# Forget gates and step sizes as extra columns of the first value products

## What is computed

```python
def fox_mixer(h, w_in, b_forget, w_out):          # the "odd" mixer, 16 heads
    q, k, v, fz = _split(h @ w_in, ODD_SPLITS)    # 1024, 1024, 1024 and 16 columns
    log_f = jax.nn.log_sigmoid(fz + b_forget)
    cum = jnp.cumsum(log_f, axis=1).transpose(0, 2, 1)
    s = einsum('bhqd,bhkd->bhqk', qc, k) * scale + cq[..., None] - cum[:, :, None, :]
    ...
def hybrid_layer(...):                            # the last mixer
    q, k, v, z, xbc, dt = jnp.split(h @ w_in, IN_SPLITS, axis=-1)   # dt has 16 columns
    attn = diff_attention(q, k, v, ...)
    ssm = ssd_mixer(z, xbc, dt, ...)              # softplus(dt + dt_bias) is the step size
```

## Time and profile before

| | us |
|---|---|
| median of 3 runs | 1215.39 (1213.45 to 1215.49) |
| the profiled execution, its time | 1214.2 |
| the profiled execution, first to last instruction (span) | 1212.4 |
| PE busy / PE weight load busy | 1180.2 / 1036.4 |
| DVE / ACT / GpSimd busy | 835.9 / 662.5 / 213.7 |
| mean granted TensorE clock, share of full speed | 0.999 |
| HBM read | 203.39 MB |
| odd mixer, from its first matmul to the first scores | 333.07 to 394.55 |
| last mixer, from its narrow product to the first scores | 883.36 to 929.68 |

### The profile page before, as it was taken

The page is one execution under the profiler, slowest core; times in us unless marked ns, Lnnn a source line. Parts: engine busy times, 40 slices in busy tenths (PEclk is TensorE's granted clock), DMA queues, the critical chain, the costliest instruction groups (busy, mean ns, idle before and its releaser), DMA issues.

```text
span 1212.4 us, 18694 instructions
## 1 busy us (share of the span) xinstructions
PE 1180.2 (97%) x7518; PEld 1036.4 (85%) x7518; DVE 835.9 (69%) x1263; ACT 662.5 (55%) x1079; POOL 213.7 (18%) x292
## 2 busy tenths in 40 slices
PE   7999999999999999999999999999999999999997
PEld 6886788888888788888888889999997689888885
DVE  6968776766586687776658876447964776777753
ACT  6528666643343766664446565445645764665641
POOL 4106422110000341220111111000002721111200
PEclk9999999999999999999999999999999999999999
DMA  7791245555453445556544454662463123554551
GB/s 286 253 250 36 104 174 193 189 209 208 144 206 141 173 139 178 200 178 215 185 191 169 179 200 140 214 213 103 146 237 106 36 79 114 191 191 175 193 194 64
DMA packets 33366, 206.05 MB, mean 170 GB/s; under 512 B 3696, under 2 KB 6272, under 8 KB 11008
## 3 DMA queue, kind: packets, MB, share of 16 engines
q1 hardware_dynamic: 29840, 200.73, 46.3%
q10 hardware_dynamic: 3440, 4.13, 1.5%
HBM read 203.39 MB, written 1.46 MB: 169 GB/s over the span
## 4 chain that ended last, share of the span: by engine, by line
PE 82%; DVE 10%; ACT 3%; DMA 3%; issue 1%; ACTq 1%; POOL 0%; DVEq 0%; POOLq 0%; SPq 0%
PE ps L671 37%; PE ps L676 19%; PE ps L688 4%; PE ps L690 4%; PE ps L689 4%; DVE wl L619 3%; DMA e_bt<-scratch 2%; PE ps L1980 2%; PE ps L1981 2%; PE ps L1982 2%; DVE tf L2395 1%; PE ps L718 1%; PE ps L720 1%; PE ps L719 1%; PE ps L941 1%
## 5 line engine op out<-in xcount | busy, mean ns | idle before, releaser
L619 DVE TENSOR_TENSOR wl<-raw,wh 128x2048 fp32r<-128x2048 f32 (+3 forms) x190 | 419.0, 2210 | 131.5 <-ACT wh L590 131.4
L590 ACT ACTIVATE wh<-raw 128x2048 fp32r<-128x2048 f32 (+2 forms) x192 | 351.0, 1831 | 147.2 <-PE ps L676 51.5
L671 PE MATMUL ps<-xb,wh 128*128 128x512 f32 x1424 | 340.9, 391 | 0.0
L671 PEld LDWEIGHTS ps<-xb,wh 128*128 128x128 f32 x1424 | 261.7, 188 | 51.5 <-issue 0.6
L676 PEld LDWEIGHTS ps<-xb,wl 128*128 128x128 f32 x1424 | 182.6, 191 | 6.9
L676 PE MATMUL ps<-xb,wl 128*128 128x256 f32 x1424 | 184.7, 283 | 0.0
L671 PE MATMUL ps<-ab,wh 128*128 128x512 f32 x640 | 156.0, 392 | 0.6 <-DVE ab L1007 0.6
L671 PEld LDWEIGHTS ps<-ab,wh 128*128 128x128 f32 x640 | 116.6, 188 | 23.5 <-DVE ab L1007 1.5
L891 DVE TENSOR_TENSOR tf<-ps,tf 128x256 f32<-128x256 f32 x148 | 62.3, 424 | 103.7 <-ACT tf L886 103.5
L886 ACT ACTIVATE tf<-ps 128x256 f32<-128x256 f32 x148 | 56.2, 382 | 121.3 <-PE ps L676 121.0
L688 PE MATMUL ps<-xb,wh 128*128 128x256 f32 x272 | 79.1, 291 | 12.9 <-DVE xb L772 10.2
(11 more groups left out here) (349 smaller groups left out, 1695.0 us busy)
## 6 DMA issues: line engine op xcount, KB each, us to landing
raw<-wstream SPq DMA_DIRECT2D x172, 1024.0 KB, 4.8
raw<-wstream SPq DMA_DIRECT2D x16, 704.0 KB, 4.1
raw<-wstream SPq DMA_DIRECT2D x4, 512.0 KB, 6.8
e_bt<-scratch ACTq DMA_DIRECT2D x16, 128.0 KB, 9.6
o_bt<-scratch SPq DMA_DIRECT2D x2, 1024.0 KB, 10.1
raw<-wstream SPq DMA_DIRECT2D x2, 560.0 KB, 10.2
raw<-wstream SPq DMA_DIRECT2D x4, 256.0 KB, 6.8
h<-xt ACTq DMA_DIRECT2D x4, 256.0 KB, 8.0
```

Source lines behind the costliest of these rows:

```text
L590: e.g.activation(WH[i % HLN][:, 0:w], RAW[i % RAWN][:, 0:w], ACT.Copy).then_inc(S["hi"], 1)
L619: e.g.tensor_tensor(WL[q][:, 0:w], RAW[i % RAWN][:, 0:w], f32(WH[q][:, 0:w]), ALU.subtract).then_inc(S["lo"], 1)
L671: e.g.matmul(two(PS[p.bank[p.unit(n)]][:, :]), WH[c % HLN][:, at * 128:at * 128 + 128], x2[:, :, tile(ks[k])], start=k == 0, stop=False, s ...
```

## The change

The 16 narrow columns are put in front of the 512 columns of the first value product: 528 columns, computed as two halves of 264 for two blocks of 128 tokens, a new kind `quad` with four PSUM banks and 96 matmuls of 264 columns. Their weights come in three chunks of 3, 3 and 2 pieces of 528 columns (before: one chunk of 8 x 16 columns and two of 4 x 512). This product moves to the front: in the odd mixer it stands in the place of `on`, with the norm's sums behind it; in the last mixer in that of `mn`. The narrow products, their transposes and drains are gone. `ok` now stands directly ahead of the odd mixer's scores, and `mk` where `mv` was. The softplus and the cumulated gates move ahead of `oq`'s drains and of `ok`; `cq` is now computed after `oq`'s drains, ahead of `ok`'s splits, and SP waits for it behind the fetches that `oq`'s events bring.

```diff
+    def quads(name, c, v):
+        for ks in ((0, 1, 2), (3, 4, 5), (6, 7)):
+            chunks.append([piece for x in ks for piece in ((name, 0, x * 128, c, 16), (name, 0, x * 128, v, 512))])
...
-        Gemm("on", "line", 16, 8, 8, "ev_dve"),
-        Gemm("oq", "cols", 8, 8, 16, "ev_dve", wide=True), Gemm("turn1", "small", 1, 0, 0, "ev_dve"),
+        Gemm("ov0", "quad", 528, 8, 3, "ev_act", fixed=(3, 4, 5, 6)),
+        Gemm("oq", "cols", 8, 8, 16, "ev_dve", wide=True),
         Gemm("ok", "cols", 8, 8, 16, "ev_dve", wide=True),
-        Gemm("ov0", "toks", 512, 8, 4, "ev_act", fixed=(5, 6)), Gemm("ov1", "toks", 512, 8, 4, "ev_act", fixed=(1, 0)),
+        Gemm("ov1", "toks", 512, 8, 4, "ev_act", fixed=(1, 0)),
...
-        Gemm("mn", "line", 16, 8, 8, "ev_dve"),
-        Gemm("mq", "cols", 4, 8, 16, "ev_dve"), Gemm("turn2", "small", 1, 0, 0, "ev_dve"),
-        Gemm("mk", "cols", 4, 8, 16, "ev_dve"),
+        Gemm("mv", "quad", 528, 8, 3, "ev_act"),
+        Gemm("mq", "cols", 4, 8, 16, "ev_dve"),
...
-        Gemm("mv", "toks", 512, 8, 4, "ev_act"),
+        Gemm("mk", "cols", 4, 8, 16, "ev_dve", fixed=(6, 0)),
...
+        def pe_quad(e, p, ready, after=None):
+            for _, k, c, at, fresh, signals in p.blocks:
+                wh, wl = pe_chunk(e, c, at)
+                ready(e, k)
+                for half in range(2):
+                    w = slice(at * 528 + half * 264, at * 528 + half * 264 + 264)
+                    for tb in range(2):
+                        u = 2 * half + tb
+                        if k == 0:
+                            e.wait(p.free[u])
+                        o, s = PS[p.bank[u]][:, 0:264], slice(k * T + tb * 128, k * T + tb * 128 + 128)
+                        e.g.matmul(o, XH[:, s], wh[:, w], start=k == 0, stop=False)
+                        e.g.matmul(o, XL[:, s], wh[:, w], start=False, stop=False)
+                        ins = e.g.matmul(o, XH[:, s], wl[:, w], start=False, stop=k == KT - 1)
...
+        def act_quad(p, dst, n, split):
+            def drain(e, u):
+                half, tb = u // 2, u % 2
+                e.wait_ge(*p.end[u])
+                e.wait_ge(S["r"], n + 1)
+                o = PS[p.bank[u]]
+                if half == 0:
+                    e.wait_ge(S["split"], split + tb + 1)
+                    src, to = o[:, 16:264], dst[tb][:, 0:248]
+                else:
+                    src, to = o[:, 0:264], dst[tb][:, 248:512]
+                e.g.activation(to, src, ACT.Copy, scale=rt(tb)).then_inc(S["ev_act"], 1)
...
+        def dve_quad(p, dst, n, bias):
+            def drain(e, u):
+                if u < 2:
+                    e.wait_ge(*p.end[u])
+                    e.wait_ge(S["r"], n + 1)
+                    e.g.scalar_tensor_tensor(out=dst[:, u * 16:u * 16 + 16], in0=PS[p.bank[u]][:, 0:16], scalar=rt(u),
+                                             in1=bias, op0=ALU.mult, op1=ALU.add).then_inc(S["split"], 1)
...
         def sp_odd(e):
-            for name in ("on", "oq", "ok"):
-                sp_gemm(e, G[name])
+            sp_gemm(e, G["ov0"])
+            sp_gemm(e, G["oq"])
             e.wait_ge(S["bt0"], 128)
             e.wait_ge(S["bt1"], 128)
             e.wait_ge(S["cq"], 1)
             e.g.dma_start(bass.AP(scratch.tensor, 0, [[T, 16], [1, T]]), TMP[1][0:16, 0:T]).then_inc(S["d_scr"], 16)
-            sp_gemm(e, G["ov0"])
+            fetch_to(e, G["ok"].first + 2)
             e.wait_ge(S["d_scr"], 32)
             for i in range(2):
                 src = bass.AP(scratch.tensor, i * 8 * T, [[0, 128], [1, 8 * T]])
                 e.g.dma_start(o_bt[i][:, :], src).then_inc(S[f"ct{i}"], 16)
+            sp_gemm(e, G["ok"])
...
         def pe_odd(e):
-            pe_narrow(e, G["on"], x_ready(2), after=pe_finish(2, [(S["r"], 2)]))
+            pe_quad(e, G["ov0"], x_ready(2), after=pe_finish(2, [(S["r"], 2)]))
             pe_cols(e, G["oq"], range(8), XB, x_ready(2))
-            pe_turn_narrow(e, G["turn1"], TMP[0], G["on"].out[0])
-            pe_cols(e, G["ok"], range(8), XB, x_ready(2))
...
-            pe_toks(e, G["ov0"], x_ready(2))
+            pe_cols(e, G["ok"], range(8), XB, x_ready(2))
```

More of the change, by code:

```diff
@@ L264, in __init__ @@
             self.tiles = [(), ()]
+        elif kind == "quad":
+            order = [(0, k, k // per, k % per) for k in range(nk)]
+            self.tiles = [(), (), (), ()]
         elif kind == "line":
@@ L367, in count @@
             if left_pair[pair(n)] == i:
-                for p in range(2) if G.kind == "toks" else (pair(n),):
+                for p in range(len(G.tiles)) if G.kind in ("toks", "quad") else (pair(n),):
                     G.end[p] = (S["gemm"], done)
@@ L898, in drain @@
                                scale=rt(tb)).then_inc(S["ev_act"], 1)
+            return drain
+        def act_quad(p, dst, n, split):
[10 more added lines that the diff above has]
+                e.g.activation(to, src, ACT.Copy, scale=rt(tb)).then_inc(S["ev_act"], 1)
+            return drain
+        def dve_quad(p, dst, n, bias):
[5 more added lines that the diff above has]
+                                             in1=bias, op0=ALU.mult, op1=ALU.add).then_inc(S["split"], 1)
             return drain
@@ L1651, in softplus_act @@
             e.g.activation(o, u, ACT.Ln).then_inc(S["sp_l"], 1)
[L1653 to L1673, removed]
         def act_odd(e):
-            act_gemm(e, G["on"], after=act_finish(2, 1e-5))
+            act_gemm(e, G["ov0"], after=act_finish(2, 1e-5), drain=act_quad(G["ov0"], o_v, 2, 0))
+            softplus_act(e, o_lf[:, :], 32, 1)
             act_gemm(e, G["oq"])
-            softplus_act(e, o_lf[:, :], 32, 1)
             act_gemm(e, G["ok"])
-            act_gemm(e, G["ov0"], drain=act_toks(G["ov0"], o_v, 0, 2))
             A = ODD
@@ L1698, in dve_odd @@
         def dve_odd(e):
[L1699 to L1702, removed]
+            dve_gemm(e, G["ov0"], 0, after=dve_finish(2, 1e-5, then=scaled(0.125)),
+                     drain=dve_quad(G["ov0"], o_ln, 2, v_("bf")))
+            e.wait_ge(S["split"], 2)
             e.link(e.g.tensor_scalar(o_ln[:, :], o_ln[:, :], -1.0, None, ALU.mult))
@@ L1707, in dve_odd @@
             e.g.tensor_scalar(o_lf[:, :], o_lf[:, :], -1.0, None, ALU.mult).then_inc(S["lf"], 1)
-            dve_gemm(e, G["ok"], 0, drain=dve_to(G["ok"], o_k, 2))
+            dve_gemm(e, G["oq"], 0, drain=dve_to(G["oq"], o_q, 2, by=3))
             e.wait_ge(S["cum"], 1)
             e.g.tensor_scalar(TMP[1][0:16, 0:T], PS[MISC][0:16, 0:T], -1.0, None, ALU.mult).then_inc(S["cq"], 1)
-            dve_gemm(e, G["ov0"], 0)
+            dve_gemm(e, G["ok"], 0, drain=dve_to(G["ok"], o_k, 2))
             dve_gemm(e, G["ov1"], 0, ahead=0)
@@ L2209, in sp_mixer @@
         def sp_mixer(e):
-            for name in ("mu", "mz", "mn", "mq", "mk", "mv", "mo"):
+            for name in ("mu", "mz", "mv", "mq", "mk", "mo"):
                 sp_gemm(e, G[name])
@@ L2274, in act_mixer @@
             act_gemm(e, G["mz"], drain=drain_z)
-            act_gemm(e, G["mn"])
-            act_gemm(e, G["mq"])
+            act_gemm(e, G["mv"], drain=act_quad(G["mv"], m_v, 5, 2))
             softplus_act(e, DT, 32, 2)
             e.g.activation(SMALL[:, 160:176], v_("alog"), ACT.Exp).then_inc(S["ea"], 1)
-            act_gemm(e, G["mk"])
+            act_gemm(e, G["mq"])
             act_decay(e, 0)
@@ L2287, in act_mixer @@
             e.g.activation(LAM[:, 0:2], LAM[:, 0:2], ACT.Exp).then_inc(S["lam_a"], 1)
-            act_gemm(e, G["mv"], drain=act_toks(G["mv"], m_v, 0, 5))
+            act_gemm(e, G["mk"])
             A = MIX
@@ L2424, in dve_mixer @@
             dve_gemm(e, G["mz"], 0, drain=drain_z)
[L2425 to L2428, removed]
+            dve_gemm(e, G["mv"], 0, drain=dve_quad(G["mv"], SMALL[:, 128:160], 5, v_("dtb")))
+            e.wait_ge(S["split"], 4)
             e.link(softplus_dve(e, DT, SMALL[:, 128:160], 32, 2, 2))
@@ L2435, in dve_mixer @@
             ins.then_inc(S["adt"], 1)
-            dve_gemm(e, G["mk"], 0, drain=dve_to(G["mk"], m_k, 5))
+            dve_gemm(e, G["mq"], 0, drain=dve_to(G["mq"], m_q, 5, by=5))
             e.wait_ge(S["adt"], 1)
@@ L2502, in dve_mixer @@
             weighted(0)
-            dve_gemm(e, G["mv"], 0)
+            dve_gemm(e, G["mk"], 0, drain=dve_to(G["mk"], m_k, 5))
             skipped(0)
@@ L2566, in pe_mixer @@
             pe_cols(e, G["mz"], range(8), XB, x_ready(5))
-            pe_narrow(e, G["mn"], x_ready(5))
+            pe_quad(e, G["mv"], x_ready(5))
             pe_cols(e, G["mq"], range(8), XB, x_ready(5))
-            pe_turn_narrow(e, G["turn2"], TMP[0], G["mn"].out[0])
-            pe_cols(e, G["mk"], range(8), XB, x_ready(5))
             o = PS[MISC]
@@ L2593, in pe_mixer @@
             pe_decay(e, 1)
-            pe_toks(e, G["mv"], x_ready(5))
+            pe_cols(e, G["mk"], range(8), XB, x_ready(5))
             pe_states(e, 0)
@@ L2719, in pe_mixer_pv @@
```

(2 more changed lines are left out.)

8 lines of the change are left out of this document (3 added, 5 removed).

## The result

The changed kernel takes 1225.3 us (median of 4 runs, 1224.43 to 1225.91); the kernel before took 1215.29 beside it. The ratio is 1.0086, 95% interval 1.0074 to 1.0098: slower by 0.86%. The prediction was 1222.5, range 1214.0 to 1227.5, 0.78 on slower. The profiled execution has a span of 1223.6, 11.2 longer than before.

The account below looks back on a forecast made before the run. PE, busy for 97% of the span, was taken as the bound. 1214.2 +7.8 (odd mixer) -3.4 (last mixer) +2.7 (clock) = 1221.3, with 1.2 from profiled execution to median 1222.5 us; range 1214.0 to 1227.5.

Parts of the forecast that it names:

- The removed work and the quad: PE's matmul work in both mixers: quad 11.7 us, odd mixer -3.2; last mixer -3.4 including its waits.
- First wait: Odd mixer, ahead of oq: its first tile needs bank 6, held by the quad's last unit until drained, +4.5 us.
- Second wait: Odd mixer, ahead of the scores: ok's drains are late behind weights queued behind o_bt, +5.8 us.
- The wait of tile 7: Odd mixer, in ok: tile 7 waits for tile 2's bank, 0.8 us.
- The clock: After a long PE wait matmuls run at 1.2 GHz: 2.7 us charged behind the second wait, nothing behind the first.
- Rival D: Odd mixer: both waits and a fall of the clock behind each, 1225.2 us, chance 0.16.
- B: Odd mixer: the queue doesn't bind, scores wait 1.3 us and the clock holds, 1214.5 us, chance 0.13.
- C: Odd mixer: the bank ahead of oq doesn't bind either, 4.5 us more goes, 1210.0 us, chance 0.09.

Follow-up runs that it names:

- The bank experiment: The changed kernel with oq's eight tiles fixed to banks 0 1 2 5 6 0 1 2, as before the change: 1218.67 us.
- The queue experiments: The changed kernel with ACT issuing the scratch write and o_bt DMAs: 1217.05 us; or with SP fetching two more chunks ahead of o_bt: 1221.1 us.
- SP's order: The changed kernel with SP fetching ok's fourth chunk and ov1's first ahead of the two o_bt DMAs: 1221.1 us.
- the kernel with the last mixer alone: The change in the last mixer only, the odd mixer as in the kernel before: 1211.59 us against 1214.88 beside it.
- The kernel with bank and queue: The changed kernel with oq's earlier banks and ACT issuing the scratch write and o_bt DMAs: 1210.06 us, 1209.79 when run once more.

## Why the prediction was right

**The removed work and the quad.** Right to 0.4. The quad took 12.09 (334.16 to 346.25) for a forecast of 11.7: 0.23 of it is the wait for bank 5, the spacing of 264 columns is 0.120 to 0.125. The last mixer gave 3.62 for 3.4, and gives it by itself.

**First wait.** Right in place, cause and size: 4.56, ended by ACT's drain of the value product. From the start of the norm's sums to `oq` it was 5.5 (346.25 to 351.74); the steps of the prediction gave 5.4. The bank experiment shows the cause.

**Second wait.** Right as well: 5.78 for 5.8. `cq` and SP's write stood 2.9 later than forecast (377.31 for 374.4: 1.1 from ahead of the mixer, 0.4 from the quad, 1.4 from the first fall), and PE with them, which leaves the wait as it is. The fourth chunk's hi copy began 14.0 after the write for a forecast of 13.0, and from its end to the scores it was 13.2 for 12.9; PE had lost 1.1 of this itself on the way. That the wait came out right to the hundredth is luck: the scores began 29.2 after SP's write for a forecast of 27.8, and PE's end of `ok` was late by the same 1.4. The wait of tile 7 was 1.21 for 0.8; with the time to refill PE, and 0.3 ahead of the fourth chunk, this pair costs 1.9 from start to start. The queue experiments show the cause: without `o_bt` in SP's queue the scores wait 1.44, and the prediction had 1.3 for that.

**The clock: the step that failed.** The prediction charged one fall of 2.7, behind the second wait alone, reasoning that 4.5 is nearer to 1.2 than to 9.0. There were two, of 1.4 and 2.8, 4.2 together. Rival D had two falls and 1225.2, with a chance of 0.16, and by the count of falls it is the case that happened; its price of 2.7 for the first fall was too high, and the bank waits and the quad made up for it. The Trainium skill ("TensorE: Matmul & The Clock Gate", section "Why this matters for your kernels") says that an idle gap within a kernel sets the array back to half its clock; the trace agrees for the gaps of 4.56 and 5.78 here and for the 4.14 of SP's order, and 1.44 left it alone. It is not the whole story: the last section shows falls with no gap over 0.5 and 1.0 in front of them. The prediction let a distance between two waits of the trace outweigh that rule, although no row spoke against it: granted clock 0.999 over a trace with no gap of this length behind its start is no evidence on what such a gap does.

**The sum.** The difference of 11.2 between the two spans is 1.1 ahead of the odd mixer, 10.85 in it up to the scores, 2.8 behind them and -3.6 in the last mixer. In the odd mixer: -2.9 for the work, with the quad as measured, +4.6 first wait, +1.4 first fall, +1.9 the bank and hi waits, +5.8 second wait, 10.8. The 1.1 belongs to no edit: the kernel with the last mixer alone has the work of the kernel before up to there, and its narrow product starts at 334.23, where the earlier trace rows have 333.07. It is a fall of the clock in the even mixer that the profiled execution of the kernel before didn't have (last section), and the 1.2 that the prediction added from that execution to the median is about its size. Against the forecast of 1222.5 the median is 2.8 too long: 1.4 the first fall, which was charged at nothing, 1.1 for tile 7 and what comes with it (1.9 for 0.8), 0.4 the quad, less 0.2 in the last mixer.

**Rivals B and C.** Neither happened, but two experiments made them true and so test their prices. B, the queue doesn't bind: 1214.5 by the text, 1217.05 measured; what it lacked is the fall behind the first wait, 2.9 there. C, the bank doesn't bind either: 1210.0 by the text, 1210.06 measured.

## What to carry to other kernels

When a product moves to the front of a stage, look at what must be known before its output can be drained, and give the next product banks that held something else. When a stage's cover moves away, follow every DMA queued behind a wait: 2 MB in front of one chunk cost 8 us here, and on ACT's queue they made nobody wait. Price a wait of TensorE of several us as the wait and a fall of the clock: behind waits of 4.1 to 5.8 us the falls here cost 1.4 to 2.9.

## What the runs showed that was not expected

The price of a fall differs where the code up to it is the same. Behind the same 4.56 us of idle time the next 16 matmuls took 5.26 in the changed kernel and 6.79 and 6.80 in the two kernels with the order of the DMAs changed: 1.4 and 2.9 over the 3.9 of full rate. Behind the second wait the fall cost 2.8 after 5.78 us, and 1.5 after 5.76 in the kernel with the bank alone. What sets it was not tried. It means that one profile can't tell the price of a fall, only that there was one. The Trainium skill ("TensorE: Matmul & The Clock Gate", section "What's actually happening") says of a kernel's start that the first matmul at full speed is not the same one in every run; here, in the middle of a kernel, it is the time until full speed is back that differs.

A fall needs no long wait, and it can come in one execution and not in another. In the even mixer the clock fell in eight of the ten profiled executions, the changed kernel's among them, and not in the kernel before's. Timeline of PE and windows of the changed kernel, then the same place of the kernel before:

```profile
88.91 1.65 PE L1509 MATMUL ps<-e_km,e_qm 64*128 64x128 f32 x8 [0.49 <-DVE e_pc L1315]
...
88.00:90.00 2.00, 1.51 (x10) 0.94 (x9) 1.38 (x6) 0.60 (x2) 0.00 (x0) 0.59 0.24 81
90.00:92.00 2.00, 2.00 (x10) 1.51 (x7) 0.66 (x5) 0.00 (x0) 0.00 (x0) 0.50 0.04 9
```

```profile
89.20 0.93 PE L1476 MATMUL ps<-e_km,e_qm 64*128 64x128 f32 x8 [0.49 <-DVE e_pc L1282]
```

The wait of 0.49 is the same in both. What PE did before it was some 30 matmuls of 15 columns (from 84.34) and a dozen small ones. In the changed kernel the stretch from these to the scores at 95.88 took 11.54, in the kernel before 8.71 (84.64 to 93.35), and of these 2.8 the odd mixer's start is 1.1 late. The kernel with bank and queue shows it without any change of code: one profiled execution had the fall and started its quad at 333.78, the other hadn't and started at 331.09. In the first the clock fell once more in the last mixer (0.52 from 956 to 958), 2 us behind a wait of 0.97. Most executions of the kernel before seem to have such falls too: of 16 beside the bank experiment, the two with a mean granted clock of 0.998 took 1212.7 and 1213.0, the seven with 0.995 1215.0 to 1215.5. Why the same code falls or doesn't was not tried. So a mean of 0.999 in one trace doesn't say that the kernel's other executions keep the clock, and differences of 1 to 3 us between two profiles can come from here.

Useless matmuls made the kernel faster: 80 of them in PE's waits took 6.1 us off the median.
